# Hybrid encoder block on eight cores: eight accumulator slots loaded a round ahead, the denominator chain issued from GpSimd, bulk loads from SyncE

## What is computed

```python
xn = rms_norm(x)
u, vg, q, k, va, gate_a, gate_b = split(xn @ w_in)
y_gmlp = gelu(u) * (W_s LN(gelu(vg)) + b)            # in chunks of 128 tokens
# three groups of 8 heads (64 wide), dilated windows (128,1), (512,4), (2048,16)
y_attn = sum over the groups g of exp-sums o_g / sum over g of denominators d_g
merged = sigmoid(gate_a) * (y_gmlp @ w_a) + sigmoid(gate_b) * (y_attn @ w_b)
h = x + merged @ w_out
h = h + (silu(hn @ w_gate) * (hn @ w_up)) @ w_down    # hn = rms_norm(h)
out = rms_norm(h)
```

## Time and profile before

| | us |
|---|---|
| median of 3 runs | 2544.25 |
| lowest and highest | 2532.6, 2562.4 |
| the profiled execution | 2554.74 |
| its span, core 6, the slowest | 2553.7 |
| spans of cores 0 to 7 | 2539.7, 2533.8, 2524.0, 2535.9, 2528.1, 2519.3, 2553.7, 2529.6 |
| TensorE matmul busy, core 6 | 2435.4 (95%) |
| VectorE, ScalarE, GpSimd busy | 1063.2, 768.8, 520.7 |

### The profile page before, as it was taken

The page is one execution under the profiler, slowest core; times in us unless marked ns, Lnnn a source line. Parts: engine busy times, 40 slices in busy tenths (PEclk is TensorE's granted clock), DMA queues, the critical chain, the costliest instruction groups (busy, mean ns, idle before and its releaser), DMA issues.

```text
span 2553.7 us, 38901 instructions; the slowest of 8 cores (2519.3 to 2553.7 us)
## 1 busy us (share of the span) xinstructions
PE 2435.4 (95%) x13248; PEld 1213.5 (48%) x13248; DVE 1063.2 (42%) x1717; ACT 768.8 (30%) x1159; POOL 520.7 (20%) x639
## 2 busy tenths in 40 slices
PE   6997899999988879999999999999999999999998
PEld 3444555555555434444444444444444444444443
DVE  4446566777666543323433433322222222323222
ACT  4445455444444412122122213222121212222111
POOL 3121201354454332222222313000000000000000
PEclk9999999999999989999999999999999999999999
DMA  9999974556666544314404517812111120201001
GB/s 212 230 248 224 226 198 117 95 110 108 132 140 133 133 153 124 98 43 124 122 19 116 132 37 189 302 34 75 50 52 71 36 75 26 83 33 67 34 34 42
DMA packets 178163, 285.75 MB, mean 112 GB/s; under 512 B 51105, under 2 KB 127521, under 8 KB 176930
## 3 DMA queue, kind: packets, MB, share of 16 engines
q1 hardware_dynamic: 133842, 203.27, 27.8%
q0 software_dynamic: 32704, 64.27, 13.6%
q10 hardware_dynamic: 11424, 15.73, 2.0%
HBM read 250.14 MB, written 104.54 MB: 139 GB/s over the span
## 4 chain that ended last, share of the span: by engine, by line
PE 77%; DMA 12%; POOL 3%; DVE 3%; issue 3%; SPq 1%; ACT 1%; ACTq 0%; DVEq 0%; POOLq 0%
PE ps L210 72%; DMA sb<-x 4%; DMA sb<-rdens 3%; PE ps L508 2%; PE ps L489 2%; DMA rdens<-sb 2%; SPq L117 1%; DMA sb<-wmx 1%; POOL sb L762 1%; POOL sb L736 1%; DMA sb<-acc 1%; PE ps L245 1%; DMA sb<-xnt 1%; DVE ps L496 1%; PE ps L1073 1%
## 5 line engine op out<-in xcount | busy, mean ns | idle before, releaser
L210 PE MATMUL ps<-sb 128*128 128x512 bf16 x10088 | 2253.1, 381 | 55.9 <-DVE sb L447 20.6
L210 PEld LDWEIGHTS ps<-sb 128*128 128x128 bf16 x10088 | 981.7, 99 | 1174.2 <-issue 87.3
L496 DVE SCALAR_TENSOR_TENSOR ps<-sb,ps 128x512 f32<-128x512 f32 x384 | 266.5, 694 | 114.4 <-PE ps L489 89.8
L1292 DVE TENSOR_TENSOR sb<-ps,sb 128x512 bf16<-128x512 f32 x176 | 121.6, 691 | 411.1 <-PE ps L210 347.0
L499 ACT ACTIVATE sb<-ps 128x1024 bf16<-128x1024 f32 x192 | 196.7, 1024 | 318.8 <-DVE ps L496 214.3
L233 POOL TENSOR_TENSOR sb<-sb 128x1 f32<-128x1 f32 x104 | 58.5, 562 | 1105.6 <-DVE sb L231 1105.6
L1291 ACT ACTIVATE sb<-ps 128x512 bf16<-128x512 f32 x176 | 105.0, 596 | 391.8 <-PE ps L210 391.8
L229 ACT ACTIVATE sb<-sb 128x1024 bf16<-128x1024 f32 x104 | 109.5, 1053 | 353.4 <-DVE sb L1307 291.8
L508 PE MATMUL ps<-sb 128*128 128x128 bf16 x1536 | 122.7, 221 | 28.7 <-DVE sb L708 18.8
L1099 DVE SCALAR_TENSOR_TENSOR sb<-sb,ps 128x512 f32<-128x512 bf16 x64 | 44.0, 688 | 245.1 <-PE ps L210 245.1
L1089 ACT ACTIVATE sb<-ps 128x512 bf16<-128x512 f32 x128 | 76.3, 596 | 228.6 <-PE ps L210 228.6
(11 more groups left out here) (65 smaller groups left out, 1017.9 us busy)
## 6 DMA issues: line engine op xcount, KB each, us to landing
sb<-x SPq DMA_DIRECT2D x72, 512.0 KB, 9.7
sb<-hres SPq DMA_DIRECT2D x64, 512.0 KB, 3.5
wfb<-wff POOLq DMA_DIRECT2D x33, 512.0 KB, 10.8
sb<-wfb SPq DMA_DIRECT2D x33, 512.0 KB, 11.0
hres<-sb SPq DMA_DIRECT2D x32, 512.0 KB, 3.8
y<-sb SPq DMA_DIRECT2D x32, 512.0 KB, 2.6
wmb<-wmx POOLq DMA_DIRECT2D x104, 128.0 KB, 4.9
sb<-xnt POOLq DMA_DIRECT2D x32, 384.0 KB, 7.0
```

The source lines that it names most:

```text
L210: tk.op("pe", lambda e: e.matmul(out, lhsT, rhs, start=start, stop=stop), R=R, W=PK(b), sig=sig)
L496: tk.op("dve", lambda e: e.scalar_tensor_tensor(out=p4, in0=m4, scalar=u["slope"][s], in1=p4, op0=ALU.mult, op1=ALU.add), R=kk + MTAB.keys ...
L1292: tk.op("dve", lambda e: e.tensor_tensor(out=AT[fc].ap, in0=PS(bks[1]), in1=sg.ap, op=ALU.mult), R=PK(bks[1]) + sg.keys, W=AT[fc].keys)
```

## The change

- **Slots.** `ACT_` has 8 slots; the four new ones lie at 154.25 to 170.25 KB. A piece's load is issued in the round before, at gu = 2: for c = 0, 1, 2 during the next-higher c of that round, for c = 3 six half-steps after the unit at c = 3. Round 0's loads stay where they were. Slots are cleared in rounds 0 and 1.
- **Chain.** The gather, the store and the broadcast are issued from POOL. The gather waits for both tiles' adds; the broadcast is one DMA instead of two. The half-steps are 2, 5, 8 and 12. The round's store `yts` stays on SP.
- **Bulk loads.** `wget` uses SP from the start. The slab is one DMA on SP, issued at once and not through `bulk`; `load_xn(0)` and `load_y(0)` go to SP.
- **Gate weights.** WGA goes into the slots freed by W1[2] and W0[2], at the start of w = 8; WGB into those of W1[0] and W1[1], in w = 8; WV into those of W0[0] and W0[1], and WU into the four new accumulator slots, both in stage 3. The feed-forward chunks follow these places.

```diff
-    ACT_ = [[bf(o + 2 * s, 2, F32) for s in range(2)] for o in (178.25, 182.25, 198.25, 186.25)]
+    ACT_ = [[bf(o + 2 * s, 2, F32) for s in range(2)]
+            for o in (154.25, 158.25, 162.25, 166.25, 178.25, 182.25, 198.25, 186.25)]
-    WV = [bf(10.25, 8), bf(18.25, 8)]
-    WU = [bf(34.25, 8), bf(42.25, 8)]
-    WGB = [bf(26.25, 8), bf(50.25, 8)]
-    WGA = [bf(154.25, 8), bf(162.25, 8)]
+    WV = [bf(34.25, 8), bf(42.25, 8)]
+    WU = [bf(154.25, 8), bf(162.25, 8)]
+    WGB = [bf(10.25, 8), bf(18.25, 8)]
+    WGA = [bf(26.25, 8), bf(50.25, 8)]
...
-    bq = dict(q="pool")
+    bq = dict(q="sp")
...
-            i = (w * 4 + c) % 4
+            i = (w * 4 + c) % 8
-                if w == 0:
+                if w < 2:
                     tk.op("pool", lambda e: e.memset(a.ap, 0.0), W=a.keys)
...
-                    if gu == 1:
-                        if c < 3:
-                            load_acc(c + 1)
-                        elif w < 7:
-                            nxt[w + 1](0)
+                    if w == 0 and gu == 1 and c < 3:
+                        load_acc(c + 1)
+                    if gu == 2 and w < 7:
+                        if c > 0:
+                            nxt[w + 1](c - 1)
+                        if c == 3:
+                            defer(6, lambda: nxt[w + 1](3))
...
-                tk.dma("sp", DEN[j].ap[64 * s:64 * s + 64, :], src.rearrange("a (p c) -> a p c", c=8),
-                       R=(ae, ao)[s].keys, W=DEN[j].keys, stream="dni%d" % j, joined=(s == 1))
+                tk.dma("pool", DEN[j].ap[64 * s:64 * s + 64, :], src.rearrange("a (p c) -> a p c", c=8),
+                       R=ae.keys + ao.keys, W=DEN[j].keys, stream="dni%d" % j, joined=(s == 1))
...
-            tk.dma("sp", rd_d[j, :, :].rearrange("a (p c) -> (a p) c", c=8), RDN[j].ap, R=RDN[j].keys, W=[("dr", "rd", j)],
+            tk.dma("pool", rd_d[j, :, :].rearrange("a (p c) -> (a p) c", c=8), RDN[j].ap, R=RDN[j].keys, W=[("dr", "rd", j)],
...
-            for s in range(2):
-                tk.dma("sp", rb.ap[64 * s:64 * s + 64, :], rd_d[j, s:s + 1, :].partition_broadcast(64), R=[("dr", "rd", j)],
-                       W=rb.keys, stream="rdi%d" % (c % 2), joined=(s == 1))
+            tk.dma("pool", rb.ap, rd_d[j].unsqueeze(1).broadcast_to([2, 64, 512]), R=[("dr", "rd", j)],
+                   W=rb.keys, stream="rdi%d" % (c % 2))
...
-            defer(1, f1)
-            defer(4, f3)
-            defer(7, f4)
-            defer(11, f5)
+            defer(2, f1)
+            defer(5, f3)
+            defer(8, f4)
+            defer(12, f5)
...
-        for i in range(4):
-            def f(i=i):
-                tk.dma("pool", s3[:, 2 * i:2 * i + 2, :], xnt_d[:, 2 * i:2 * i + 2, lo:lo + 768], R=R,
-                       W=s.keys[12 * i:12 * i + 12], stream="slab%d" % (w % 2), joined=(i > 0))
-            bulk.append(f)
+        tk.dma("sp", s3[:, :, 0:768], xnt_d[:, :, lo:lo + 768], R=R, W=s.keys, stream="slab%d" % (w % 2))
...
             if w == 8:
                 if i == 0:
                     for hf in range(2):
-                        wget(WGB[hf], CH_GB + hf, "wgb%d" % hf)
+                        wget(WGA[hf], CH_GA + hf, "wga%d" % hf)
...
                 if i in (5, 9):
-                    wget(WV[i // 9], CH_V + i // 9, "wv%d" % (i // 9))
-                if i == 12:
-                    wget(WU[0], CH_U, "wu0")
+                    wget(WGB[i // 9], CH_GB + i // 9, "wgb%d" % (i // 9))
...
             if w == 6 and i == 0:
-                for hf in range(2):
-                    wget(WGA[hf], CH_GA + hf, "wga%d" % hf)
...
         if oc == 0:
-            wget(WU[1], CH_U + 1, "wu1")
+            for hf in range(2):
+                wget(WV[hf], CH_V + hf, "wv%d" % hf)
+        if oc == 6:
+            for hf in range(2):
+                wget(WU[hf], CH_U + hf, "wu%d" % hf)
```

More of the change, by code:

```diff
@@ L304, in build_program @@
     T2B = [bf(202.25 + 2 * i, 2, F32) for i in range(2)]
-    slots = ([10.25 + 4 * i for i in range(4)] + [34.25 + 4 * i for i in range(4)] + [154.25 + 4 * i for i in range(4)]
+    slots = ([34.25 + 4 * i for i in range(4)] + [154.25 + 4 * i for i in range(4)] + [10.25 + 4 * i for i in range(4)]
              + [26.25, 30.25, 50.25, 54.25] + [70.25 + 4 * i for i in range(4)] + [178.25, 182.25, 66.25]
@@ L658, in g01_units @@
         for c in range(4):
-            i4 = (w * 4 + c) % 4
+            i4 = (w * 4 + c) % 8
             for gu in range(4):
@@ L964, in load_xn @@
     def load_xn(t):
-        tk.dma("sp" if t else "pool", XN2[t % 2].ap.rearrange("p (k t) -> p k t", k=8), xnt_d[:, :, t * T:(t + 1) * T],
+        tk.dma("sp", XN2[t % 2].ap.rearrange("p (k t) -> p k t", k=8), xnt_d[:, :, t * T:(t + 1) * T],
                R=[("dr", "xnt", t)], W=XN2[t % 2].keys, stream="xnl%d" % (t % 2 if t else 2))
@@ L971, in load_y @@
     def load_y(t):
-        tk.dma("sp" if t else "pool", YB.ap.rearrange("p (c t) -> p c t", c=4), yt_d[t], R=[("dr", "yt", t)], W=YB.keys, stream="yl" if t else "yl0")
+        tk.dma("sp", YB.ap.rearrange("p (c t) -> p c t", c=4), yt_d[t], R=[("dr", "yt", t)], W=YB.keys, stream="yl" if t else "yl0")
     for w in range(9):
```

## The result

The changed kernel is slower: its executions took 2671.49, 2668.22 and 2677.62 us, against 2532.6, 2544.25 and 2562.4 us before, a ratio of 1.0495 (95% interval 1.0391 to 1.0599). I had predicted 2516 us, in 2503 to 2556. In some executions of either kernel the cores of one die show a lower granted clock throughout; all times and ratios here leave these out.

What follows compares the result with a forecast made beforehand. The serial denominator chain was taken as the bound, at 14.7 us a step. Its terms summed to 12.95, giving 2508.6 us, just under TensorE's 2514.4; with 2 us for the last round, 2516, 8 in 10 within 2503 to 2556.

Steps and rivals of the forecast that it cites:

- the broadcast's term: Chain step, broadcast issue to next multiply: one DMA instead of two, put at 5.6 us, between 4.03 and 6.1.
- Multiply to reciprocal: Chain step on GpSimd: 3.15 us (2.87 to 3.43), with a cast issue between in about half of the pieces.
- Reciprocal to store: Chain step on GpSimd: 1.7 us, taken as the same operation as before.
- Store to broadcast: Chain step, store now issued from GpSimd: 2.5 us, between 1.56 and 4.9.
- The likeliest case: Second stretch: chain hidden behind TensorE's work, its step at 12.95 us under the meeting point 13.14; 2516 us, chance 0.53.
- rival 1: Denominator chain stays the bound and slots help nothing: step about 13.3 to 15 us, 2519 to 2570 us; chance 0.33.
- rival 3: Gate weights late: WGA's last piece waits behind a yts store, first gates 10 to 15 us later, about 2530; chance 0.04.
- rival 2: GpSimd's queue, shared by chain DMAs and casts, lengthens the step: 16.1 us, 2603 us; chance 0.10 for over 15 us.
- The formula 2120.1 + 30 L: Chain's limit on the whole time in us, with L the chain's step from multiply to multiply, predicted at 12.95.
- TensorE's limit: Whole kernel if TensorE's work sets the time: 450.4 + 403 + 41.9 + 1619.1 = 2514.4 us.
- The eight slots: Accumulator loads a round ahead: VectorE's 34.2 us of waits go unless the chain falls over 33 + 42 us behind.
- Bulk loads and gate weights: Loads on SyncE's queue and moved weights: hidden, with 30 us or more of cover unless the chain lags that much.

Runs made afterwards that it cites:

- e11: Kernel before, its two broadcasts split by columns (256 to all 128 rows each) instead of rows; ratio 1.0442 to the kernel before.
- e1: Changed kernel with the broadcast again as two DMAs of 64 rows, both still issued by GpSimd; ratio 1.0037 to the kernel before, profiled at 2541.4 us.
- e2: Kernel before with its two broadcasts made one DMA of the [2, 64, 512] source, still from SyncE; ratio 1.0432 to the kernel before.
- e8: Changed kernel, one broadcast kept, with the multiply deferred to position 14 instead of 12 (last piece 7 instead of 4); ratio 1.0403 to the kernel before.
- e4: e3 with the multiply deferred to position 13 instead of 11, behind the next piece's reciprocal (last piece at 6); ratio 0.9934 to the kernel before.
- e10: e8 with the two gathers of a piece issued by SyncE instead of GpSimd; ratio 1.0210 to the kernel before.
- e3: Changed kernel with gathers, store and two 64-row broadcasts back on SyncE; slots, bulk loads and gate weights as changed; ratio 0.9964 to the kernel before.
- e7: e4 with the slabs in four pieces and the gate weights back on GpSimd's queue; ratio 0.9959 to the kernel before.
- e9: e5 with the two gathers of a piece issued by SyncE instead of GpSimd; ratio 0.9966 to the kernel before.
- e5: e1 with the multiply deferred to position 14 instead of 12 (last piece at 7); ratio 1.0060 to the kernel before.

## Why the prediction was wrong

**The failed step is the broadcast's term.** I took 5.6 us from broadcast to multiply, between 4.03 and 6.1; it measured 9.19 on core 2. Both bounds came from broadcasts of 64 rows, and for the old form itself 6.1 was no upper bound: the mean of this term was 6.4 us on core 5 and 7.0 on core 6. GpSimd's other broadcast of twice the size landed in 4.6, so I read "one DMA instead of two" as a saved issue. I compared bytes and queues and never asked how the new access pattern is divided. e11 shows the bounds had to be taken from a row with the same outermost size, and the trace of before has none. The Trainium skill's rule on outermost sizes, named under e11 with its page, speaks against this very edit; I had drawn on the fixed cost of a GpSimd DMA and not that rule.

**The other terms, on core 2.** Multiply to reciprocal took 3.12 (3.15 predicted), which was right. Reciprocal to store took 2.26 (1.7): GpSimd waits 0.56 to 0.59 (28 of 31 times; else up to 0.76) after its own reciprocal before it issues the store that reads it, where SyncE issued 1.73 after the start of a reciprocal of 1.67, 0.06 after its end. Store to broadcast took 3.72 (2.5), inside the bounds of 1.56 to 4.9 but 1.2 short, with a landing of 1.8 at the median and up to 8.3. Together they are 3.12 + 2.26 + 3.72 + 9.19 = 18.3.

**The likeliest case would have failed anyway.** With the broadcasts in their old form (e1) the terms are 3.15 + 2.27 + 3.67 + 5.33 = 14.4 on core 0: the broadcast is under my 5.6, the two around the store are over by 1.7, and the step stays above 13.14. That is rival 1, "the chain stays the bound", with about its numbers (13.3 to 15, 2519 to 2570): 14.4 gives 2552, the span is 2540. In e1 TensorE also waits 14.1 us for a gate weight on core 0, which is what rival 3 had (10 to 15). What came is the side of rival 2, a longer step on GpSimd, but not by its mechanism: its 16.1 had casts landing behind one another, and its share of 0.10 and end of 2603 were too small.

**What held.**

- The formula 2120.1 + 30 L. With the median step over the cores it gives 2664 against a slowest span of 2670 for the change (2669 with core 2's own step), 2645 against 2636 for e2, 2642 against 2647 for e8, 2656 against 2657 for e11, 2519 against 2519 for e4. Only e10 lies well above it, 2564 against 2590; a wait of 38.4 us for a gate weight is among its TensorE waits, and it was not followed up.
- TensorE's limit of 2514.4. The cores of e4 end at 2504 to 2519.
- The eight slots. With the chain in time (e3, e4) VectorE's 34.2 us are gone; in the changed kernel two waits with 38.7 us came back on core 2, the longest 29.3, since the loads stood behind a yts store held by the late multiplies. That is the condition I had named for SyncE's queue, a chain over 30 us late, and not the one for the slots, 33 + 42 us. The first of the two waits is at the 18th piece, at 676.7. Its load was issued at 671.6, right behind a yts store that had waited for the multiply of the 12th piece at 668.2, which came 72 us after that piece's adds where the first piece's came 18 after; its slot was free from 638.4 on.
- Bulk loads and gate weights. With the chain in time they cost next to nothing: the slowest core of e3 waits for none, that of e7 3.2 us. The waits for weights and slabs in the changed kernel, 48.2 and 41.7 us, are the chain's lateness passed on through SyncE's queue. Slots and gate weights were not run one at a time.

**What I had not seen in the order.** Slots do not shorten a serial step (e3: 13.5 to 14.0 us); moving the multiply behind the next reciprocal did (e4: 13.22 to 13.44), though it gained little time. The prediction had named the loop, "the reciprocal of a piece stands on GpSimd behind the multiply of the piece before", and treated it as given.

## What to carry to other kernels

Before two DMAs are merged into one, look at the outermost size of both access patterns: two of 64 rows were done 4.5 us after the first issue, one of [2, 64] rows after 8.1, with the same bytes on the same queue. Where a chain's time is steps times length, cost the loop that closes it, member by member and queue by queue, and ask whether another order or queue cuts it: here it took two positions of a multiply with the chain on SyncE (e4), and the gather's queue as well with the chain on GpSimd (e9). And see whether the step sets the pace at all, or only the end. And a load that has 30 us of cover has it only as long as whatever stands ahead of it in its queue is on time.

## What the hardware showed that I had not expected

GpSimd's queue was not slower than SyncE's for such broadcasts: from the first issue, a pair was done in 4.5 us from GpSimd in e1 and in 5.6 from SyncE in e3 (medians, core 0 of both), and after the reorder in 4.9 from either (e5, core 1; e4, core 4). A narrow transfer also delays small ones behind it, in two of their 16 updates: the last four of two gathers' 32 updates came 3.3 us after the other 28 in the changed kernel, and 0.04 us after in e1. And GpSimd mostly pays 0.56 to 0.59 us between its own reciprocal and the store that reads it. VectorE's bf16 copies are not seen to hold up GpSimd's issues: 98 cast issues in 440 to 1030 us of the changed kernel took 552 ns in the mean, about as before (a median of 561); the part of rival 2 that rested on longer issues did not happen.
